# Casting all weights of a hybrid decoder step to bf16 in DRAM first, and streaming every tile from there

## The reference, cut to what matters

```python
def layer(x, ...):
    x = x + 0.5 * rmsnorm(swiglu(rmsnorm(x, n_ffn1_pre), ffn1_wg, ffn1_wu, ffn1_wd), n_ffn1_post)
    mix, new = mixer(rmsnorm(x, n_mix_pre), ...)
    x = x + rmsnorm(mix, n_mix_post)
    x = x + 0.5 * rmsnorm(swiglu(rmsnorm(x, n_ffn2_pre), ffn2_wg, ffn2_wu, ffn2_wd), n_ffn2_post)

swiglu(x, wg, wu, wd) = (silu(x @ wg) * (x @ wu)) @ wd

def mixer(u, ...):
    rg_x, rg_g, z, xbc, dt, g_rg, g_ssd = split(u @ w_in)       # 1024 x 10272
    h    = RG-LRU(causal_conv(rg_x));  y_rg = h * gelu(rg_g)     # scan over time
    y    = chunked SSD scan(silu(causal_conv(xbc)), dt) + D skip
    y_ssd = grouped_rmsnorm(y * silu(z)) * w
    m    = sigmoid(g_rg) * (y_rg @ w_proj_rg) + sigmoid(g_ssd) * (y_ssd @ w_proj_ssd)
    return m @ w_out
```

## Time and profile before

| | us |
|---|---|
| shown runs, median of 2 | 4505.82 |
| shown runs, lowest and highest | 4413.99 and 4597.65 |
| the profiled execution, slowest core | 4426.94 |
| its span, from first to last instruction | 4425.9 |
| spans of the other cores | 4389.2 to 4409.2 |

### The profile page before, as it was taken

The page is one execution under the profiler, slowest core; times in us unless marked ns, Lnnn a source line. Parts: engine busy times, 40 slices in busy tenths (PEclk is TensorE's granted clock), DMA queues, the critical chain, the costliest instruction groups (busy, mean ns, idle before and its releaser), DMA issues.

```text
span 4425.9 us, 45835 instructions; the slowest of 8 cores (4389.2 to 4425.9 us)
## 1 busy us (share of the span) xinstructions
PE 2684.6 (61%) x13227; PEld 1331.7 (30%) x13399; DVE 1892.6 (43%) x3421; ACT 1324.4 (30%) x2903; POOL 158.4 (4%) x207
## 2 busy tenths in 40 slices
PE   4545745565685745876857458768574577434544
PEld 1221322222231322333313223333132233223433
DVE  1025767220126677322266772222667722125551
ACT  1025522120225622122255221222562212135111
POOL 1100100011000000000000000000000000000000
PEclk8767877887797977988979779889797798755666
DMA  8943910799331300242313002423130024245646
GB/s 169 178 93 79 180 39 1 121 178 181 141 117 38 116 1 1 100 171 110 114 39 115 1 1 100 170 111 114 39 115 1 1 100 166 72 180 175 179 125 221
DMA packets 201062, 459.10 MB, mean 104 GB/s; under 512 B 13154, under 2 KB 134890, under 8 KB 169997
## 3 DMA queue, kind: packets, MB, share of 16 engines
q1 hardware_dynamic: 54720, 321.00, 19.9%
q0 software_dynamic: 113072, 118.38, 15.6%
q10 hardware_dynamic: 33024, 16.78, 1.4%
HBM read 429.05 MB, written 91.62 MB: 118 GB/s over the span
## 4 chain that ended last, share of the span: by engine, by line
PE 38%; DVE 25%; DMA 17%; issue 9%; ACT 8%; DVEq 1%; POOL 1%; ACTq 0%; another core or an unknown queue 0%; POOLq 0%; SPq 0%
PE bank L353 35%; DMA ring<-wg 6%; DVE arena L471 4%; DMA ring<-wscr 3%; PE bank L356 3%; DMA ring<-win 2%; DVE sst L758 2%; DVE arena L758 2%; DVE xnb L375 1%; DVE arena L807 1%; DVE arena L806 1%; DVE arena L465 1%; DVE arena L790 1%; ACT xnb L369 1%; DVE arena L809 1%
## 5 line engine op out<-in xcount | busy, mean ns | idle before, releaser
L353 PE MATMUL bank<-xnt,ring 128*128 128x512 bf16 (+1 forms) x5970 | 1268.4, 374 | 195.2 <-DMA ring<-wu 123.4
L353 PEld LDWEIGHTS bank<-xnt,ring 128*128 128x128 bf16 x6080 | 567.8, 109 | 853.4 <-issue 376.9
L353 PE MATMUL bank<-arena 128*128 128x512 bf16 (+5 forms) x2663 | 441.8, 312 | 154.5 <-DMA arena<-wd 49.0
L427 DVE TENSOR_TENSOR arena<-arena,bank 128x512 bf16<-128x512 f32 x182 | 124.9, 686 | 764.9 <-PE bank L353 650.6
L471 DVE SCALAR_TENSOR_TENSOR arena<-arena,pf 128x512 f32<-128x512 f32 (+1 forms) x600 | 395.0, 658 | 64.4 <-DVE arena L471 1.4
L353 PEld LDWEIGHTS bank<-arena 128*128 128x128 bf16 (+3 forms) x2688 | 231.0, 102 | 445.4 <-issue 278.2
L426 ACT ACTIVATE arena<-bank 128x512 f32<-128x512 f32 x182 | 108.5, 596 | 679.8 <-PE bank L353 667.5
L353 PE MATMUL bank<-arena,const 128*128 128x512 f32 (+2 forms) x340 | 187.5, 648 | 195.9 <-DVE arena L779 107.3
L353 PE MATMUL bank<-arena,ring 128*128 128x512 bf16 (+1 forms) x940 | 206.6, 375 | 83.2 <-DMA ring<-wscr 42.0
L356 PE MATMUL bank<-idb,xnb 128*128 128x128 bf16 (+1 forms) x408 | 50.3, 302 | 329.1 <-DVE xnb L375 327.4
L356 PE MATMUL bank<-idb,arena 128*128 128x128 bf16 (+2 forms) x680 | 75.1, 272 | 200.1 <-DVE arena L826 139.9
(11 more groups left out here) (162 smaller groups left out, 3275.2 us busy)
## 6 DMA issues: line engine op xcount, KB each, us to landing
ring<-wscr SPq DMA_DIRECT2D x192, 1024.0 KB, 5.4
wscr<-ring SPq DMA_DIRECT2D x48, 1024.0 KB, 7.3
arena<-wdscr SPq DMA_DIRECT2D x88, 512.0 KB, 6.3
arena<-sss POOLq DMA_DIRECT2D x16, 1024.0 KB, 9.6
o_sss<-arena ACTq DMA_DIRECT2D x16, 1024.0 KB, 6.1
nw<-nv POOLq DMA_DIRECT2D x30, 512.0 KB, 6.6
ring<-win POOLq DMA_DIRECT2D x12, 1024.0 KB, 13.0
ring<-wg POOLq DMA_DIRECT2D x22, 512.0 KB, 15.1
```

What stands on the lines that cost most here:

```text
L353: return pe.op(lambda h: h.matmul(out, lhsT, rhs, start=start, stop=stop), reads, [bk.b], inc=stop)
L427: V(lambda h: h.tensor_tensor(out=HT.t[:, fc0:fc0 + nb, :].rearrange("p a b -> p (a b)"), in0=sg.t[:, 0:W_], in1=pu.t[:, 0:W_], op=ALU.mul ...
```

## The change

All casts are issued on POOL ahead of everything else that it does except the two loads of RG-LRU weights (`emit_casts`), straight from the float32 weights in DRAM to the bf16 scratch in DRAM, in the order in which the first tile uses them. The ring and the wd pieces are then loaded from the scratch by SP in every tile, the first included. Since POOL's queue now begins with all the casts, the `io` transfers of the first prompt tile are issued by ACT (`IOH[0] = act`), and by POOL again after it. ACT's transfers get 8 semaphores in place of 4.

```diff
@@ Kern
-        self.act = Eng(self, nc.scalar, "act", ndma=4)
+        self.act = Eng(self, nc.scalar, "act", ndma=8)
@@ build
-    io = pool
+    IOH = [pool]
...
+    def emit_casts():
+        for r in range(NB):
+            for ii, (off, nk, ncols, src_ap) in enumerate(tile_seq[r]):
+                dst = SCR[r, :, off:off + nk * ncols].rearrange("p (k c) -> p k c", k=nk)
+                pool.dma(dst, src_ap, writes=[SCRB[r]], add=(ii > 0))
+            fi = 0 if r < 11 else (1 if r >= NB - 11 else None)
+            if fi is not None:
+                j = r if fi == 0 else r - (NB - 11)
+                pool.dma(WDS[fi, j].rearrange("p (k c) -> p k c", k=2), wd[fi][j * 256:(j + 1) * 256, :].rearrange("(k p) c -> p k c", p=128),
+                         writes=[WDSB[fi][j]])
@@ wnext
-            if r < NB or ntiles == 1:
-                for ii, (off, nk, ncols, src_ap) in enumerate(seq[r]):
-                    dst = slot.t[:, off:off + nk * ncols].rearrange("p (k c) -> p k c", k=nk)
-                    pool.dma(dst, src_ap, writes=[slot.b], add=(ii > 0))
-                if ntiles > 1:
-                    sp.dma(SCR[r, :, 0:used], slot.t[:, 0:used], reads=[slot.b], writes=[SCRB[r]])
-            else:
-                sp.dma(slot.t[:, 0:used], SCR[r % NB, :, 0:used], reads=[SCRB[r % NB]], writes=[slot.b])
+            sp.dma(slot.t[:, 0:used], SCR[r % NB, :, 0:used], reads=[SCRB[r % NB]], writes=[slot.b])
@@ wd_load
-        if first:
-            pool.dma(dst.t[:], wd[fi][j * 256:(j + 1) * 256, :].rearrange("(k p) c -> p k c", p=128), writes=[dst.b])
-            if ntiles > 1:
-                sp.dma(WDS[fi, j], d2, reads=[dst.b], writes=[WDSB[fi][j]])
-        else:
-            sp.dma(d2, WDS[fi, j], reads=[WDSB[fi][j]], writes=[dst.b])
+        sp.dma(d2, WDS[fi, j], reads=[WDSB[fi][j]], writes=[dst.b])
@@ load_nw, the cdscr transfers of the mixer, and all others that were io.dma
-        io.dma(...)
+        IOH[0].dma(...)
@@ end of build
+    emit_casts()
     for v in (RGC, HC, XBCC, S):
...
     for ti in range(NPT):
         t0 = ti * 512
+        if ti == 0:
+            IOH[0] = act
...
+        IOH[0] = pool
```

More of the change, by code:

```diff
@@ L335, in wd_load @@
     def wd_load(fi, j, dst):
-        first = wd_tile[fi] < 11
-        wd_tile[fi] += 1
         d2 = dst.t[:].rearrange("p k c -> p (k c)")
-        if first:
-            pool.dma(dst.t[:], wd[fi][j * 256:(j + 1) * 256, :].rearrange("(k p) c -> p k c", p=128), writes=[dst.b])
-            if ntiles > 1:
-                sp.dma(WDS[fi, j], d2, reads=[dst.b], writes=[WDSB[fi][j]])
-        else:
-            sp.dma(d2, WDS[fi, j], reads=[WDSB[fi][j]], writes=[dst.b])
+        sp.dma(d2, WDS[fi, j], reads=[WDSB[fi][j]], writes=[dst.b])
     def A(fn, r, w):
@@ L362, in load_nw @@
         nwi[0] += 1
-        io.dma(nw.t[:], nv[idx:idx + 1, :].partition_broadcast(128).rearrange("p a b -> p (a b)"), writes=[nw.b])
+        IOH[0].dma(nw.t[:], nv[idx:idx + 1, :].partition_broadcast(128).rearrange("p a b -> p (a b)"), writes=[nw.b])
         return nw
@@ L605, in mixer @@
         A(lambda h: h.activation(out=TOT.t[0:32, 0:J], in_=bk.t[0:32, 0:J], func=AF.Exp), [bk.b], [TOT.b])
-        io.dma(CDSCR[:, 0:J], TOT.t[0:32, 0:J], reads=[TOT.b], writes=[CDSB])
+        IOH[0].dma(CDSCR[:, 0:J], TOT.t[0:32, 0:J], reads=[TOT.b], writes=[CDSB])
         for qh in range(2):
             src_ap = CDSCR.rearrange("(hc two) j -> two hc j", two=2)[qh][:, 0:J].unsqueeze(0).broadcast_to([64, 16, J])
-            io.dma(CDa.t[qh * 64:(qh + 1) * 64, :, :], src_ap, reads=[CDSB], writes=[CDa.b], add=(qh > 0))
+            IOH[0].dma(CDa.t[qh * 64:(qh + 1) * 64, :, :], src_ap, reads=[CDSB], writes=[CDa.b], add=(qh > 0))
         XSBs = [AR.alloc("xsb%d" % i, [128, T_], BF16) for i in range(4)]
@@ L683, in mixer @@
             MKB = AR.alloc("maskb", [128, 1024], F32)
-            io.dma(MKB.t[:], maskb_d, writes=[MKB.b])
+            IOH[0].dma(MKB.t[:], maskb_d, writes=[MKB.b])
             MASKB = MKB.t
@@ L718, in sL @@
                 if nseq > 1:
-                    io.dma(S0[b % 3].t[:], sss[b].rearrange("(hc q) n -> q hc n", q=128), writes=[S0[b % 3].b])
+                    IOH[0].dma(S0[b % 3].t[:], sss[b].rearrange("(hc q) n -> q hc n", q=128), writes=[S0[b % 3].b])
             def sA(b):
@@ L907, in build @@
         t0 = ti * 512
-        io.dma(X.t[:, :, :], xp[t0:t0 + 512, :].rearrange("(s p) d -> p s d", p=128), writes=[X.b])
+        if ti == 0:
+            IOH[0] = act
+        IOH[0].dma(X.t[:, :, :], xp[t0:t0 + 512, :].rearrange("(s p) d -> p s d", p=128), writes=[X.b])
         ffn(0, 512, 128, 4, 0, 1)
@@ L911, in build @@
         ffn(1, 512, 128, 4, 4, 5)
-        io.dma(yp[t0:t0 + 512, :].rearrange("(s p) d -> p s d", p=128), X.t[:, :, :], reads=[X.b])
+        IOH[0].dma(yp[t0:t0 + 512, :].rearrange("(s p) d -> p s d", p=128), X.t[:, :, :], reads=[X.b])
+        IOH[0] = pool
     W0, W1, W2 = alloc_stg()
-    io.dma(o_pss.rearrange("(hc q) n -> q hc n", q=128), S.t[:], reads=[S.b])
+    IOH[0].dma(o_pss.rearrange("(hc q) n -> q hc n", q=128), S.t[:], reads=[S.b])
     bk = K.bank()
@@ L918, in build @@
     A(lambda h: h.activation(out=STG[0].t[0:8, 0:128], in_=bk.t[0:8, 0:128], func=AF.Copy), [bk.b], [STG[0].b])
-    io.dma(o_prh, STG[0].t[0:8, 0:128], reads=[STG[0].b])
-    fm_to_rows(lambda c: (RGC.t[:, c, 0:3], RGC.b), 8, 3, W1, lambda st: io.dma(o_prc, st.t[0:3, 0:1024], reads=[st.b]))
-    fm_to_rows(lambda c: (XBCC.t[:, c, 0:3], XBCC.b), 32, 3, W0, lambda st: io.dma(o_psc, st.t[0:3, 0:4096], reads=[st.b]))
+    IOH[0].dma(o_prh, STG[0].t[0:8, 0:128], reads=[STG[0].b])
+    fm_to_rows(lambda c: (RGC.t[:, c, 0:3], RGC.b), 8, 3, W1, lambda st: IOH[0].dma(o_prc, st.t[0:3, 0:1024], reads=[st.b]))
+    fm_to_rows(lambda c: (XBCC.t[:, c, 0:3], XBCC.b), 32, 3, W0, lambda st: IOH[0].dma(o_psc, st.t[0:3, 0:4096], reads=[st.b]))
     if DO_SAMPLE:
@@ L925, in build @@
         for t in range(4):
-            io.dma(X.t[t * 16:(t + 1) * 16, 0, :], xs[:, t, :], writes=[X.b], add=(t > 0))
+            IOH[0].dma(X.t[t * 16:(t + 1) * 16, 0, :], xs[:, t, :], writes=[X.b], add=(t > 0))
         def rows_to_fm(load_fn, nrows, nchunks, dst, TMw):
@@ L939, in ld_rows3 @@
             for t in range(3):
-                io.dma(TMw.t[t * 16:(t + 1) * 16, 0:w], srcd[:, t, :], writes=[TMw.b], add=(t > 0))
+                IOH[0].dma(TMw.t[t * 16:(t + 1) * 16, 0:w], srcd[:, t, :], writes=[TMw.b], add=(t > 0))
         rows_to_fm(lambda TMw: ld_rows3(src, TMw, 1024), 48, 8, RGC, W1)
-        rows_to_fm(lambda TMw: io.dma(TMw.t[0:16, 0:1024], srh, writes=[TMw.b]), 16, 8, HC, W2)
+        rows_to_fm(lambda TMw: IOH[0].dma(TMw.t[0:16, 0:1024], srh, writes=[TMw.b]), 16, 8, HC, W2)
         rows_to_fm(lambda TMw: ld_rows3(ssc, TMw, 4096), 48, 32, XBCC, W0)
@@ L949, in build @@
         for t in range(4):
-            io.dma(ys[:, t, :], X.t[t * 16:(t + 1) * 16, 0, :], reads=[X.b])
+            IOH[0].dma(ys[:, t, :], X.t[t * 16:(t + 1) * 16, 0, :], reads=[X.b])
         W0, W1, W2 = alloc_stg()
-        fm_to_rows(lambda c: (HC.t[:, c, 0:16], HC.b), 8, 16, W2, lambda st: io.dma(o_srh, st.t[0:16, 0:1024], reads=[st.b]))
+        fm_to_rows(lambda c: (HC.t[:, c, 0:16], HC.b), 8, 16, W2, lambda st: IOH[0].dma(o_srh, st.t[0:16, 0:1024], reads=[st.b]))
         def st3(dst, st, w):
             for t in range(3):
-                io.dma(dst[:, t, :], st.t[t * 16:(t + 1) * 16, 0:w], reads=[st.b])
+                IOH[0].dma(dst[:, t, :], st.t[t * 16:(t + 1) * 16, 0:w], reads=[st.b])
         fm_to_rows(lambda c: (RGC.t[:, c, 0:48], RGC.b), 8, 48, W1, lambda st: st3(o_src, st, 1024))
```

## The result

The changed kernel takes 4820.8 us (median), 9.2% more than the kernel before: ratio 1.0921, 95% interval 1.0881 to 1.0961. The forecast was 4366. The profiled execution took 4819.06 us, its span on core 6 is 4818.0, and all eight cores lie between 4796.6 and 4818.0, so whatever it is strikes them alike.

The account below looks back on a forecast made before the run. The prediction took the casts to bound both FFNs of tile 0. Sum: 4427 − 83 (FFN2) − 31 (mixer) + 53 (FFN1) = 4366 us, with 8 in 10 runs from 4308 to 4430.

Parts of the forecast that it names:

- the one on FFN1: FFN1 of tile 0: PE waits for 19.5 MiB of casts, 13 batches, then two loads; +53 us, ends +4 and +82.
- The slower rival: Last block of FFN2, tile 0: casting below 60 GB/s bounds the tile; about 4767 us at half rate; chance 0.08.
- the 750 that I had named for its landing: Sign to check in tile 0: the last cast should land by 750 us.
- FFN2 of tile 0: All casts done by about 724 us, before FFN2 starts, so it takes 142.1 us as in tile 1: −83.
- Mixer: Mixer of tile 0: −48 from loading blocks from the scratch, +17 for three added costs; sum −31, ends −39 and −18.
- The decays: Mixer of tile 0: ACT issues three chunk-decay transfers and stands still for two landings; 10 us, ends 5 and 17.
- The norm weights: Mixer of tile 0: issued only when ACT gets there, they may be late beside casts; 2 us.
- A cast into DRAM, beside the tile's loads: FFN1 of tile 0: each 1.573 MB batch pays a lone store's cost for the DRAM write; +3.8 us, 13 batches, 49.
- FFN1 in all: FFN1 of tile 0: net +4 from waits and earlier casting, plus 49 for casts into DRAM; +53 us.
- the head start: FFN1 of tile 0: casting starts some 8 us sooner, as X and the norm weights no longer stand before it.
- The price of 207 GB/s: Skill page's DRAM-to-DRAM rate per direction; read so, a batch costs +6.7 us and the sum would be 4404.
- the cheap rival: Casts in FFN1, tile 0: writing to DRAM costs at most +1.7 us a batch; 4311 to 4338 us; chance 0.27.

Follow-up runs that it names:

- the repaired kernel: The changed kernel, but in the first tile the arena's snapshot leaves the casts' semaphores out; 4369.8 us, ratio 0.9887 to the kernel before.
- The cap alone: The kernel before, with the ring's lookahead ending at FFN1's last block while FFN1 of the first tile runs; ratio 0.9934.
- e2: The changed kernel with the casts recorded inside the first FFN, after its arena buffers are made, POOL's queue the same; 4747.9 us, ratio 1.0740.
- e4: The kernel before, with only X, norm weights and chunk decays of the first prompt tile issued by ACT, and its 8 semaphores; ratio 1.0044.

## Why the prediction was wrong

**The step that failed** is the one on FFN1: "Here the casts stay on the path, with 11 x 1.5 MiB to move and 3 MiB of mixer blocks between them." I asked which data PE waits for, and listed 19.5 MiB. ACT waited for 61 MiB, none of which it reads. The snapshot was in the code that I had, and in the order of the calls, but a wait that comes from how memory is handed out shows in no list of data. The trace of before has it, in small:

```profile
566.15 1.28 ACT L698 ACT_TABLE_LOAD   x1 [6.98 <-DMA wscr<-ring]
569.56 0.19 DVE L699 TENSOR_TENSOR arena<-arena 128x32 f32<-128x32 f32 x1 [11.26 <-DMA ring<-win]
...
953.17 1.28 ACT L426 ACT_TABLE_LOAD   x1 [5.11 <-DMA ring<-wg]
```

All three write into the arena and read nothing of the ring, yet a store or a cast of a ring slot is what they wait for last. The third is the very Silu that stood still for 660.8 us, here at the start of FFN2. They stand behind whatever was recorded ahead of the snapshot and had not landed, and in that kernel this is at most a few blocks. In the repaired kernel, where no slot is stored any more and the snapshot leaves POOL's casts out, ACT's gap before the first of them is 0.9 us in place of 7.0.
I also wrote that no cast waits for the tile, and didn't ask the opposite, which instructions of the tile wait for POOL's counts. It cost 454.7 us in FFN1 (818.5 against 363.8 in the repaired kernel).

**The slower rival** had the sign and nearly the size (4767) by the wrong mechanism. It needed less than 60 GB/s of casting. The casts ran at 64.0 MB in 694 us, 92 GB/s, close to the 90 I took, and were done at 706.7 us against my 724. That was beside an idle tile, though. In the repaired kernel the last cast was only issued at 797.3 us, later than the 750 that I had named for its landing, and still long before FFN2 at 966.8.

**The other terms held in the main**, as the repaired kernel shows against the kernel before:

- FFN2 of tile 0: −83 forecast, −82.9 in the changed kernel.
- Mixer: −31 forecast, −30.4 (603.0 against 633.4). The decays cost 11.5 for the 10 taken. The norm weights were later than I took: PE's first transposes begin 12.2 us after the squares in place of 7.5, 4.8 for the 2 taken.
- A cast into DRAM, beside the tile's loads: +3.8 us a batch forecast. The wu casts of the repaired kernel start at 100.97 and, seven blocks on, at 252.46: 21.6 us a block against 18.0, +3.6. In the DMA views of such stretches (100 to 252 us, and 84 to 192 before) the packets of POOL's casts took 65.5% of the engines' time for 11.01 MB and 65.8% for 9.44 MB. That is 14.2 us a batch against 11.8, so 2.4 of the 3.6 is engine time of the casts themselves. What the write alone costs was not isolated.

```profile
100.97 0.88 POOL L108 DMA_DIRECT2D wscr<-wu  x1 [17.12 <-DMA wscr<-wg]
...
252.46 0.88 POOL L108 DMA_DIRECT2D wscr<-wu  x1 [20.08 <-DMA wscr<-wg]
```

- FFN1 in all: +53 forecast, +66.5 in the repaired kernel. Of the missing 13, 8 are the head start that did not come. X left POOL's queue but shared the engines with the first cast from ACT's, and wu was issued at 34.5 us, not earlier than before.

The price of 207 GB/s that the Trainium skill has for copies in DRAM ("DMA: Bandwidth & Descriptors", section "Latency and other measured facts"), which would have meant +6.7 a batch by my estimate, is not borne out. In the changed kernel a stretch with casts alone reaches 201 GB/s written in its best slice, which is 402 GB/s read, and 101 written as a mean with its gaps (DMA view, 500 to 700 us, slices of 5 us):

```profile
GB/s 89 110 105 113 175 118 99 26 175 72 47 119 143 51 89 180 45 85 170 59 61 158 96 43 109 157 25 76 201 28 72 170 64 70 148 97 51 124 139 60
```

The row of the Trainium skill is for copies on the queues of SP and ACT, with a pitch of 512 KiB from row to row. These copies differ in both and in the cast, so it may be right for its own. One term of my range can't be rebuilt: the cheap rival's 4311 lies below the 4317 that the sum gives at no cost at all.

## What to carry to other kernels

Before work is moved ahead in program order, look for everything that takes "all that was issued so far" as its condition: snapshots of semaphores, resets of an arena, barriers. The moved work joins each of them, however little it has to do with them, and what was meant to run in the background becomes a barrier. Then ask what stands behind the moved or waiting step in each queue: here two such waits (SP behind the casts of the next stage, ACT behind three small transfers) were worth some 24 and 13 us. With them and the false wait gone, and FFN1's weights cast straight into the ring as before, casting the rest ahead gives 3.3%. The cap alone gives 0.7% without any of it.

## What the runs showed of the hardware

Two things I had not expected. First, three small transfers on ACT's own queue take very different times beside other traffic: from the first issue to the next work of ACT 7.1 and 7.6 us with no casts in flight (e2 and the changed kernel), 11.5 and 21.8 to 27.1 with them, though nothing stands before them in their queue. They are made of small pieces: the DMA view of e4, 450 to 490 us, has 0.03 MB in 2122 packets on ACT's queue q10.

```profile
q0 software_dynamic: 3783, 3.81, 66.5%
q1 hardware_dynamic: 576, 4.19, 34.8%
q10 hardware_dynamic: 2122, 0.03, 5.4%
```

Why they take long was only seen, not tested. Second, keeping up to 12 casts in flight in place of three raised the busy share of the engines from 0.85 to 1.04 by the windows view but not the rate by much: a block took 20.0 us in place of 21.6, and the ring loads beside them 13.3 us to land in place of 8.2.
